# Low halves moved to GpSimd in three places, keys projected ahead of queries, and two heads alternating in an attention product, in a one-core float32 program of three transformer blocks

## The chip, the cores and the metric

The kernel runs on 1 core of one Trainium2 chip. The metric is device microseconds of one execution. Before the change three runs took 3091.12, 3094.21 and 3099.16 us, with a median of 3094.21.

## The reference

Everything is float32, with 256 tokens and a width of 1024. The first block is one layer with four branches, merged by gates, and a gated feed-forward network:

```
h = rms(x)
y_fox = softmax(q k / 8 + cum_f[q] - cum_f[k], causal) v    # 16 heads of 64, "forgetting" attention
y_lru = RG-LRU(h)                                           # a convolution and a linear recurrence
y_sb  = stick-breaking attention(h)                         # 16 heads of 64
y_mem = attention(h, 256 memory tokens)                     # 4 heads of 256
x += (sum_n sigmoid(h Wg_n) * (y_n Wb_n)) Wout
x += (silu(conv(h2 W1)) * (h2 W2)) Wdown
```

The second block has two layers over two streams, the 256 tokens and 256 context tokens, with shifts and scales from a modulation vector (ada):

```
h, hc = modulate(rms(x)), modulate(rms(ctx))
q, k, v, ... = split(h @ w_in), and the same of hc          # in the last layer hc gives only keys and values
ya = neighbourhood attention(q; keys of ctx and of x)       # 8 heads of 64, 512 keys
yb = differential attention(q; keys of ctx and of x)        # 4 heads of 2 x 64, 512 keys
yc = gMLP(u, v)
x += gate * merge(ya, yb, yc);   in layer 0 also ctx += ...
x += gate * mixture of 16 experts(x);  in layer 0 also for ctx
```

## The kernel before

One program of five instruction streams (TensorE `pe`, ScalarE `act`, VectorE `dve`, GpSimd `pool`, SyncE), written out by hand from line 2350 on. They meet at a barrier (`barrier`, L408) between stages: each stream drains, adds 1 to `stage_done`, and waits until all four have. The stages in their order: loads and norm; Q, K and V of the forgetting attention; its rounds; the recurrence; stick-breaking; memory; the first merge; the output projection; the feed-forward network; then for each layer the projection of K, Q and V (`proj2`), neighbourhood attention, in layer 0 context attention, differential attention (in layer 0 again for the context), gMLP, merge, output, router, experts.

**Weights.** They come as 621 slots of 1 MB through `ring`, four slots of two pieces (128 x 1024 words). SyncE issues a slot's load when both of its old pieces have been reported used. Most pieces are multiplied in three fp32r matmuls so that the result is as exact as float32 (`three`): high half times high half, high times low, low times high. So each such piece takes three steps: ScalarE rounds it to its high half (`split_hi`, L421, into one of four buffers `piece_hi`), VectorE subtracts to get the low half (`split_lo`, L428, into `ring_lo`), TensorE multiplies (L481 to L483; `piece_of` waits for the low half). 378 pieces are split so; the experts' pieces are not.

**Order.** Nothing is scheduled by a program: each stream's order is the order of the code. `split_ahead` is called on ScalarE and VectorE each time a piece is passed (`next_piece`), and puts the halves of the pieces up to `AHEAD = 3` further at that point of the stream. Both streams pass a piece at the read of its bank (`read_bank`), whichever of them reads it. So VectorE's low half stands between a bank's read and what comes next, and waits there for ScalarE's high half. GpSimd has little to do: it issues its own loads at some barriers, makes four products for the forgetting attention's mask and bias (L1133), adds squares in norms (L893) and low halves of the routed activations (L2094).

**Attention rounds.** A round is two heads (64 rows of the array each) and 256 queries in two tiles. `att_pe` runs on TensorE, per round: `scores` (L657), `turn` (transposes of the probabilities, L672), `product` with V (L682), and at two places a piece or two of other projections (`also`). On the others: ScalarE's exponentials (L726) and copies of the transposed (L741), VectorE's maxima (L787), reciprocals (L792) and probabilities (L796; in differential attention L799 subtracts the second map). The forgetting rounds are written apart (L1154 to L1234; L1173 is their product, L1234 their probabilities), 8 rounds of two heads. Differential attention has 4 rounds a layer and stream, neighbourhood attention 4.

**The layers' first stage, `proj2`.** `main_norm_dve` normalises the columns chunk by chunk (8 chunks of 128 rows): L938 scales, L944 gives the low half, of each of the two streams of 256 columns. `first_banks` takes three pieces at once, chunk by chunk of the norm (`ready`). Then one bank a piece (`fm_banks`), and last V (`tm_tile`). Queries came first: four banks of 512 columns in layer 0, of 256 in layer 1 (the context has no queries there), then four banks of keys of 512 columns. In layer 1 the norm of the context stream was made after the first chunks, between the banks of Q (`second_chunk_dve`, `norm_hi_act`), and TensorE waited for it ahead of K (`both`).

## Time and profile before

| | |
|---|---|
| three runs | 3091.12, 3094.21, 3099.16 us |
| profiled execution | 3091.37 us |
| its span | 3089.2 us |
| mean granted TensorE clock | 0.944 |
| TensorE busy | 2607.8 us, 84% of the span |
| VectorE busy | 1175.6 us, 38% |
| ScalarE busy | 877.1 us, 28% |
| GpSimd busy | 90.4 us, 3% |
| DMA | 669.40 MB, mean 217 GB/s |
| stages the change touches, us from the span's start | forgetting rounds 139.1 to 219.9; first merge 457.4 to 690.4; layer 0 proj2 931.4 to 1013.9, neighbourhood attention to 1097.4, context to 1140.1, differential to 1201.8, the same for the context to 1240.8; layer 1 proj2 2130.0 to 2215.4, neighbourhood attention to 2321.1, differential to 2380.5 |

How to read it: the span is the time from the first to the last instruction of the profiled execution, and its own time lies 2.2 us above it. Busy times are sums over an engine's instructions. A wait in the trace is idle time just before an instruction, put down to what came last before it; L numbers are lines of the kernel. A group of rows "x16" is as many instructions, and its time is from the first one's start to the last one's end. Matmuls are pipelined and overlap in the records. One float32 matmul of the attention rounds leaves two records.

### The profile page before, as it was taken

The numbers are of one execution on the slowest core, as the hardware profiler recorded it, in microseconds if no ns is written. First come the engines' busy times: TensorE is split into PE (matmuls) and PEld (weight loads), VectorE is DVE, ScalarE is ACT, GpSimd is POOL, SyncE is SP. The second block draws the span as 40 slices with busy tenths as digits, with TensorE's granted clock in tenths as the row PEclk, the third lists the DMA queues.
The fourth block names the chain that finished last, engine by engine and source line by source line (L and its number), as shares of the span: only waits on it lengthen the run. The fifth ranks groups of instructions, "written<-read, shape, count | busy, mean of one in ns | idle before, by whom it ended". The sixth has DMA issues, their size and how long they took to land.

```text
span 3089.2 us, 37382 instructions
## 1 busy us (share of the span) xinstructions
PE 2607.8 (84%) x14760; PEld 1784.8 (58%) x14760; DVE 1175.6 (38%) x1628; ACT 877.1 (28%) x1348; POOL 90.4 (3%) x78
## 2 busy tenths in 40 slices
PE   5889989999998988899787778886897987778786
PEld 5688868888996677588552222223676973222222
DVE  4557534456754645544430001014355651000001
ACT  4455533344443333322220000003234431000001
POOL 1100000000010000000110000001000001000000
PEclk8899989999999999899979999998898988999999
DMA  4434217764542111122469999995212435999996
GB/s 160 149 123 164 99 66 272 268 235 143 186 159 108 62 52 55 42 95 96 160 240 417 400 399 392 416 410 213 73 64 79 160 141 242 413 405 411 419 409 271
DMA packets 92949, 669.40 MB, mean 217 GB/s; under 512 B 10320, under 2 KB 10496, under 8 KB 12800
## 3 DMA queue, kind: packets, MB, share of 16 engines
q1 hardware_dynamic: 90256, 654.67, 54.1%
q0 software_dynamic: 2272, 11.52, 1.1%
q8 instruction: 115, 1.88, 0.2%
q10 hardware_dynamic: 272, 1.05, 0.1%
q14 instruction: 34, 0.28, 0.0%
HBM read 666.13 MB, written 1.06 MB: 216 GB/s over the span
## 4 chain that ended last, share of the span: by engine, by line
PE 44%; DMA 27%; DVE 7%; ACT 4%; issue 3%; DVEq 1%; SPq 0%; POOL 0%; ACTq 0%; POOLq 0%; PEldq 0%; PEld 0%
DMA ring<-in_stream 27%; PE ps L481 10%; PE ps L483 10%; PE ps L482 10%; PE ps L2186 7%; PE ps L496 2%; ACT piece_hi L421 1%; PE ps L682 1%; DVE WK L796 1%; DVE ring_lo L428 1%; ACT WK L726 1%; DVE small L787 1%; PE ps L672 1%; PE ps L657 1%; PE ps L494 1%
## 5 line engine op out<-in xcount | busy, mean ns | idle before, releaser
L2186 PE MATMUL ps<-ring,WK 128*64 128x512 f32 x3072 | 728.3, 603 | 167.0 <-DMA ring<-in_stream 143.2
L481 PE MATMUL ps<-A,piece_hi 128*128 128x256 f32 (+1 forms) x1952 | 624.3, 320 | 72.2 <-DVE A L944 26.4
L428 DVE TENSOR_TENSOR ring_lo<-ring,piece_hi 128x1024 fp32r<-128x1024 f32 x378 | 466.1, 1237 | 450.0 <-ACT piece_hi L421 449.1
L482 PE MATMUL ps<-A,piece_hi 128*128 128x256 f32 (+1 forms) x1952 | 610.8, 313 | 0.0
L483 PE MATMUL ps<-A,ring_lo 128*128 128x256 f32 (+1 forms) x1952 | 609.8, 312 | 0.0
L2186 PEld LDWEIGHTS ps<-ring,WK 128*64 128x64 f32 x3072 | 193.6, 136 | 667.7 <-DMA ring<-in_stream 370.5
L421 ACT ACTIVATE piece_hi<-ring 128x1024 fp32r<-128x1024 f32 x378 | 391.9, 1053 | 271.7 <-DMA ring<-in_stream 109.3
L481 PEld LDWEIGHTS ps<-A,piece_hi 128*128 128x128 f32 x1952 | 383.3, 196 | 116.2 <-issue 82.1
L482 PEld LDWEIGHTS ps<-A,piece_hi 128*128 128x128 f32 x1952 | 383.9, 197 | 18.3
L483 PEld LDWEIGHTS ps<-A,ring_lo 128*128 128x128 f32 x1952 | 382.6, 196 | 18.5
L2306 DVE TENSOR_TENSOR WK<-WK,ps 128x512 f32<-128x512 f32 x32 | 22.0, 687 | 630.1 <-PE ps L2186 630.1
L481 PE MATMUL ps<-WKR,piece_hi 128*128 128x256 f32 (+1 forms) x624 | 188.6, 302 | 4.7 <-DVE WKR L589 2.6
L482 PE MATMUL ps<-WKR,piece_hi 128*128 128x256 f32 (+1 forms) x624 | 187.5, 300 | 0.0
L483 PE MATMUL ps<-WKR,ring_lo 128*128 128x256 f32 (+1 forms) x624 | 187.4, 300 | 0.0
L2272 ACT ACTIVATE WK<-ps 128x512 f32<-128x512 f32 x32 | 19.1, 597 | 552.3 <-PE ps L2186 552.2
L481 PE MATMUL ps<-piece_hi,A 128*128 128x256 f32 (+1 forms) x480 | 158.7, 331 | 5.2 <-DVE WK L1851 5.2
L482 PE MATMUL ps<-ring_lo,A 128*128 128x256 f32 (+1 forms) x480 | 155.5, 324 | 0.0
L483 PE MATMUL ps<-piece_hi,A 128*128 128x256 f32 (+1 forms) x480 | 155.2, 323 | 0.0
L2254 DVE COPY WK<-ps 32x512 f32<-32x512 f32 x48 | 32.7, 682 | 272.1 <-PE ps L2186 271.9
L481 PEld LDWEIGHTS ps<-WKR,piece_hi 128*128 128x128 f32 x624 | 119.9, 192 | 18.7 <-issue 15.1
L483 PEld LDWEIGHTS ps<-WKR,ring_lo 128*128 128x128 f32 x624 | 120.1, 192 | 3.8
L482 PEld LDWEIGHTS ps<-WKR,piece_hi 128*128 128x128 f32 x624 | 120.0, 192 | 3.8
(266 smaller groups left out, 2433.1 us busy)
## 6 DMA issues: line engine op xcount, KB each, us to landing
ring<-in_stream SPq DMA_DIRECT2D x621, 1024.0 KB, 7.7
WK<-in_na_bias POOLq DMA_DIRECT2D x2, 2048.0 KB, 8.0
WK<-cum_scratch POOLq DMA_DIRECT2D x1, 2048.0 KB, 9.5
const<-in_const SPq DMA_DIRECT2D x1, 1267.0 KB, 12.0
WK<-in_x SPq DMA_DIRECT2D x1, 1024.0 KB, 5.5
WK<-in_mem SPq DMA_DIRECT2D x1, 1024.0 KB, 9.4
WK<-cum_scratch POOLq DMA_DIRECT2D x1, 1024.0 KB, 14.3
WK<-in_lru_w POOLq DMA_DIRECT2D x1, 1024.0 KB, 5.9
```

Of the source, the lines that this page charges most:

```text
L421: nc.scalar.activation(piece_hi[:, no % 4, :], ring[:, slot, at:at + PIECE], ACT.Copy).then_inc(hi_done[no % 4], 1)
L428: nc.vector.tensor_tensor(ring_lo[:, slot, at:at + PIECE], ring[:, slot, at:at + PIECE], f32(piece_hi[:, no % 4, :]), ALU.subtract).then_i ...
L481: nc.tensor.matmul(out_, l[0], r[0], start=first, stop=False)
L482: nc.tensor.matmul(out_, l[0], r[1], start=False, stop=False)
L483: return nc.tensor.matmul(out_, l[1], r[0], start=False, stop=last)
L494: last = nc.tensor.transpose(ps[0:rows, b, at:at + n], l, r)
L496: last = nc.tensor.matmul(ps[0:rows, b, at:at + n], l, r, start=(k == 0), stop=(k == len(pairs) - 1))
L657: last = nc.tensor.matmul(dst[:, a, qt, :], l, m, start=(j == 0), stop=(j == len(pairs) - 1))
L672: last = nc.tensor.transpose(ps[:, b, col % 512:col % 512 + P], t[:, a, qt, k * P:(k + 1) * P], ident)
L682: last = nc.tensor.matmul(ps[rows, at["y_bank"] + col // 512, col % 512:col % 512 + T], l, m, start=(j == 0), stop=(j == len(pairs) - 1))
L2186: last = nc.tensor.matmul(ps[64 * n:64 * n + 64, bank, :], lhs, piece[:, n * 512:n * 512 + 512], start=(k == 0), stop=(k == DC - 1))
L2254: return copy(YE[row:row + CAP, s, e // 4, half * 512:half * 512 + 512], ps[64 * half + CAP * s:64 * half + CAP * (s + 1), 6 + e % 2, :])
```

## The change

1. A table `GPS_LOW` marks 120 of the 378 split pieces, by their number among the split: 24 to 39 (the forgetting rounds), 88 to 151 (the first merge), and 20 in each layer, from the 13th split piece of the layer on (keys and queries of differential attention, 4 of its values, 8 of the gates). VectorE and ScalarE go past them as before, but GpSimd makes their low halves. `lows` does this in its stream: at each barrier it first makes those that ScalarE had made high halves of by that barrier (`ahead_of`), and at two places of each layer it is called ahead of a wait.
2. `att_pe`: in the score loop the query tile is the outer loop. In the product two heads take turns (`heads_beside=2`), matmul by matmul, for the attention of pairs; differential and memory attention keep one head after the other (`heads_beside=1`).
3. `proj2`: the norm always makes both streams, keys come first, then queries, then values; the stream of weights has the same order. `second_chunk_dve` and the norm between the banks of Q are gone.

```diff
+GPS_LOW = np.zeros(PIECES + 64, bool)
+def _mark_low():
+    split = np.array(SPLIT_AT)
+    block = 226
+    layer = MIX_PIECES
+    for lo, hi in ((24, 40), (88, 152), *((block + l * layer + 12, block + l * layer + 32) for l in range(LAYERS))):
+        GPS_LOW[split[lo:hi]] = True
...
         def barrier(eng, cur):
+            if cur.who == "act":
+                ahead_of.append(cur.s)
+            if cur.who == "pool":
+                lows(eng, cur)
             eng.drain().then_inc(stage_done, 1)
...
-        def split_lo(dve, cur):
+        def split_lo(eng, cur):
...
+            if cur.who == "dve":
+                nc.vector.tensor_tensor(to, of, hi, ALU.subtract).then_inc(lo_done[no % 4], 1)
+            else:
+                nc.gpsimd.tensor_tensor(to, of, hi, ALU.subtract).then_inc(lo_done[no % 4], 1)
             cur.s += 1
+        def lows(pool, cur):
+            while cur.s < ahead_of[cur.stage]:
+                if GPS_LOW[cur.s]:
+                    split_lo(pool, cur)
+                else:
+                    cur.s += 1
...
                 elif cur.who == "dve":
-                    split_lo(eng, cur)
+                    if GPS_LOW[cur.s]:
+                        cur.s += 1
+                    else:
+                        split_lo(eng, cur)
...
-                for a in range(2):
-                    for qt in range(2):
+                for qt in range(2):
+                    for a in range(2):
...
-                for a, rows, col, pairs in at["pv"](r):
-                    for j, (l, m) in enumerate(pairs):
-                        last = nc.tensor.matmul(ps[rows, at["y_bank"] + col // 512, col % 512:col % 512 + T], l, m,
-                                                start=(j == 0), stop=(j == len(pairs) - 1))
+                parts = at["pv"](r)
+                width = at["heads_beside"]
+                for at_ in range(0, len(parts), width):
+                    for j in range(kc):
+                        for rows, col, pairs in parts[at_:at_ + width]:
+                            last = nc.tensor.matmul(ps[rows, at["y_bank"] + col // 512, col % 512:col % 512 + T], *pairs[j],
+                                                    start=(j == 0), stop=(j == kc - 1))
...
-        def proj2_pe(pe, cur, nq, ready, both):
-            first_banks(pe, cur, in_a()(nq), nq, ready)
-            fm_banks(pe, cur, in_a()(nq), nq, BC - 3)
-            both()
-            fm_banks(pe, cur, in_a()(2 * T), 2 * T, BC)
+        def proj2_pe(pe, cur, nq, ready):
+            first_banks(pe, cur, in_a()(2 * T), 2 * T, ready)
+            fm_banks(pe, cur, in_a()(2 * T), 2 * T, BC - 3)
+            fm_banks(pe, cur, in_a()(nq), nq, BC)
             tm_tile(pe, cur, 0, 4)
-        def proj2_read(eng, who, cur, nq, beside):
-            for c in range(BC):
-                copies(eng, who, cur, lambda j: Q2[:, j, 0:nq], 1, nq, HD ** -0.5, first=c)
-                beside(c)
+        def proj2_read(eng, who, cur, nq):
             copies(eng, who, cur, lambda j: K2[:, j, :], 4, 2 * T)
+            copies(eng, who, cur, lambda j: Q2[:, j, 0:nq], 4, nq, HD ** -0.5)
             copies(eng, who, cur, lambda j: V2[:, j, :], 4, BW, tm=True)
...
                 barrier(pool, cur)
+                lows(pool, cur)
                 pool.wait_ge(loads, 16 * (n_loads + 1))
                 barrier(pool, cur)
...
+                lows(pool, cur)
                 pool.wait_ge(loads, 16 * (n_loads + 4))
```

VectorE in a forgetting round, where L1221 adds the bias to the scores, L1223 and L1224 take the maxima, L1231 and L1234 make the probabilities, L576 copies a bank of other projections. Before:

```order
L1221 TENSOR_TENSOR WK<-ps,WK 128x768
L1223 TENSOR_REDUCE small<-WK 128x2
L1224 TENSOR_REDUCE small<-WK 128x2
L428 TENSOR_TENSOR ring_lo<-ring,piece_hi 128x1024
L1231 RECIPROCAL small<-small 128x4
L1234 TENSOR_TENSOR WK<-WK,small 128x2x256
L1234 TENSOR_TENSOR WK<-WK,small 128x2x128
L576 TENSOR_SCALAR WK<-ps 128x256
L428 TENSOR_TENSOR ring_lo<-ring,piece_hi 128x1024
```

VectorE in the same round now (the code's lines have moved by 36 to 40):

```order
L1261 TENSOR_TENSOR WK<-ps,WK 128x768
L1263 TENSOR_REDUCE small<-WK 128x2
L1264 TENSOR_REDUCE small<-WK 128x2
L1271 RECIPROCAL small<-small 128x4
L1274 TENSOR_TENSOR WK<-WK,small 128x2x256
L1274 TENSOR_TENSOR WK<-WK,small 128x2x128
L612 TENSOR_SCALAR WK<-ps 128x256
```

Both low halves have left VectorE's round; nothing else of it moved.

GpSimd from the mask and bias of the forgetting attention to the load for the context (`L1127` to `L2688` before). Before:

```order
L1127 DMA WK<-cum_scratch 128x16x128
L1133 TENSOR_TENSOR WK<-WK,const 128x4x256 x4
L2681 DMA WK<-in_lru_w 128x2048
L2688 DMA WK<-in_ctx 128x2x1024
```

GpSimd there now:

```order
L1167 DMA WK<-cum_scratch 128x16x128
L1173 TENSOR_TENSOR WK<-WK,const 128x4x256 x4
L454 TENSOR_TENSOR ring_lo<-ring,piece_hi 128x1024 x16
L2709 DMA WK<-in_lru_w 128x2048
L454 TENSOR_TENSOR ring_lo<-ring,piece_hi 128x1024 x64
L2716 DMA WK<-in_ctx 128x2x1024
```

L454 is GpSimd's low half. Sixteen stand behind the four products, the first three of them ahead of the barrier before the forgetting rounds, and 64 ahead of the merge's end. In the layers 11 and 9 such rows stand in layer 0, and 15 and 5 in layer 1, on the two sides of the loads for the gMLP.

VectorE in layer 1's `proj2`, from the norm's reciprocal (L954 before) on. Before:

```order
L954 RECIPROCAL WK<-WK 128x512
L938 SCALAR_TENSOR_TENSOR WK<-XT,gmod,WK 128x256 x2
L944 SCALAR_TENSOR_TENSOR A<-WK,MOD,A 128x256
...
L944 SCALAR_TENSOR_TENSOR A<-WK,MOD,A 128x256 x2
L428 TENSOR_TENSOR ring_lo<-ring,piece_hi 128x1024
L938 SCALAR_TENSOR_TENSOR WK<-XT,gmod,WK 128x256 x2
L944 SCALAR_TENSOR_TENSOR A<-WK,MOD,A 128x256
L576 TENSOR_SCALAR WK<-ps 128x256
L428 TENSOR_TENSOR ring_lo<-ring,piece_hi 128x1024
L938 SCALAR_TENSOR_TENSOR WK<-XT,gmod,WK 128x256
L944 SCALAR_TENSOR_TENSOR A<-WK,MOD,A 128x256
```

VectorE there now:

```order
L994 RECIPROCAL WK<-WK 128x512
L978 SCALAR_TENSOR_TENSOR WK<-XT,gmod,WK 128x256 x4
L984 SCALAR_TENSOR_TENSOR A<-WK,MOD,A 128x256 x2
L978 SCALAR_TENSOR_TENSOR WK<-XT,gmod,WK 128x256 x2
...
L984 SCALAR_TENSOR_TENSOR A<-WK,MOD,A 128x256 x4
L452 TENSOR_TENSOR ring_lo<-ring,piece_hi 128x1024
L612 TENSOR_SCALAR WK<-ps 128x512
L452 TENSOR_TENSOR ring_lo<-ring,piece_hi 128x1024 x2
L612 TENSOR_SCALAR WK<-ps 128x512
```

The norm of the second stream (L938 and L944 of it) has moved from behind and between the first banks' reads to their front, two instructions of each kind for a chunk; the first read is now of a bank of 512 columns.

## Rows read from the trace of the kernel before

**Rows 1.** The page: busy time, share, instructions; and one costly group of instructions

```profile
PE 2607.8 (84%) x14760; PEld 1784.8 (58%) x14760; DVE 1175.6 (38%) x1628; ACT 877.1 (28%) x1348; POOL 90.4 (3%) x78
L428 DVE TENSOR_TENSOR ring_lo<-ring,piece_hi 128x1024 fp32r<-128x1024 f32 x378 | 466.1, 1237 | 450.0 <-ACT piece_hi L421 449.1
```

**Rows 2.** Stretches: us; PE, PEld, DVE, ACT, POOL busy; clock, DMA share, GB/s

```profile
139.10:219.90 80.80, 70.56 (x560) 63.84 (x560) 45.84 (x72) 42.27 (x105) 0.00 (x0) 0.92 0.26 93
457.40:690.40 233.00, 220.79 (x1752) 195.46 (x1752) 114.11 (x139) 85.98 (x102) 0.00 (x0) 0.98 0.67 250
931.40:1013.90 82.50, 69.93 (x292) 56.14 (x292) 34.91 (x52) 24.26 (x36) 0.56 (x1) 0.94 0.27 101
2130.00:2215.40 85.40, 63.68 (x292) 52.77 (x292) 34.92 (x52) 24.58 (x36) 0.55 (x1) 0.84 0.25 88
```

**Rows 3.** PE's waits (total, times, longest): forgetting, merge 1-2, context, differential 0, neighbourhood 1, differential 1

```profile
PE ps L1165 <- DVE WK L1234: 8.5, 6, 5.4
...
PE ps L481 <- DVE ring_lo L428: 5.3, 9, 0.8
PE ps L1733 <- DVE ROWS L1769: 4.4, 2, 2.3
...
PE ps L672 <- DVE WK L796: 3.6, 2, 2.4
...
PE ps L672 <- DVE WK L799: 8.4, 4, 4.2
...
PE ps L481 <- DVE WK L1851: 5.2, 1, 5.2
...
PE ps L672 <- DVE WK L799: 8.1, 4, 4.2
```

**Rows 4.** PE's timeline in layer 1's proj2: start, us, engine, instruction, [idle before]

```profile
2140.65 0.55 PE L481 MATMUL ps<-A,piece_hi 128*128 128x256 f32 x1 [7.92 <-DVE A L944]
...
2153.49 0.36 PE L481 MATMUL ps<-A,piece_hi 128*128 128x256 f32 x1 [2.15 <-DVE ring_lo L428]
...
2167.33 0.80 PE L481 MATMUL ps<-A,piece_hi 128*128 128x512 f32 x1 [9.60 <-DVE A L944]
...
2213.01 0.39 PE L483 MATMUL ps<-piece_hi,A 128*128 128x512 f32 x1
```

**Rows 5.** PE's timeline in layer 0's proj2, first and last matmuls

```profile
942.23 0.77 PE L481 MATMUL ps<-A,piece_hi 128*128 128x512 f32 x1 [8.84 <-DVE A L944]
...
962.65 0.47 PE L481 MATMUL ps<-A,piece_hi 128*128 128x512 f32 x1 [1.72 <-DVE ring_lo L428]
...
1011.28 0.39 PE L482 MATMUL ps<-ring_lo,A 128*128 128x512 f32 x1
1011.51 0.39 PE L483 MATMUL ps<-piece_hi,A 128*128 128x512 f32 x1
```

**Rows 6.** PE's timeline: product and scores of neighbourhood attention, product of a forgetting round

```profile
1044.21 2.86 PE L682 MATMUL ps<-WK 128*64 128x256 f32 x16
1047.01 1.99 PE L657 MATMUL ps<-WK 64*128 64x512 f32 x8
...
152.90 0.87 PE L1173 MATMUL ps<-WK 128*64 128x256 f32 x8
```

**Rows 7.** GpSimd (timeline; a group) and VectorE (timeline) with two operands of SBUF

```profile
121.42 12.32 POOL L1133 TENSOR_TENSOR WK<-WK,const 128x1024 f32<-128x1024 f32 x4 [13.17 <-DMA WK<-cum_scratch]
...
L2094 POOL TENSOR_TENSOR A<-WK,A 128x1024 fp32r<-128x1024 f32 x6 | 14.4, 2433 | 75.5 <-ACT A L2079 75.5
...
122.10 6.15 DVE L428 TENSOR_TENSOR ring_lo<-ring,piece_hi 128x1024 fp32r<-128x1024 f32 x2 [2.32 <-ACT piece_hi L421]
```

**Rows 8.** ACT's and VectorE's timeline in a differential round of layer 0

```profile
1149.13 1.07 ACT L421 ACTIVATE piece_hi<-ring 128x1024 fp32r<-128x1024 f32 x1
...
1149.75 2.29 DVE L796 TENSOR_TENSOR WK<-WK,small 128x2048 f32<-128x2048 f32 x1
```

**Rows 9.** VectorE's timeline in a forgetting round

```profile
172.49 1.22 DVE L428 TENSOR_TENSOR ring_lo<-ring,piece_hi 128x1024 fp32r<-128x1024 f32 x1 [3.15 <-ACT piece_hi L421]
```

More of the change, by code:

```diff
@@ L422, in split_hi @@
             cur.s += 1
[L424 removed]
+        def split_lo(eng, cur):
             no, slot, at = int(SPLIT_NO[cur.s]), cur.s // 2 % R, cur.s % 2 * PIECE
[L427 to L430 removed]
+            eng.wait_ge(hi_done[no % 4], cur.split_use(cur.s, 1))
+            to, of, hi = ring_lo[:, slot, at:at + PIECE], ring[:, slot, at:at + PIECE], f32(piece_hi[:, no % 4, :])
+            if cur.who == "dve":
+                nc.vector.tensor_tensor(to, of, hi, ALU.subtract).then_inc(lo_done[no % 4], 1)
+            else:
+                nc.gpsimd.tensor_tensor(to, of, hi, ALU.subtract).then_inc(lo_done[no % 4], 1)
+            cur.s += 1
+        def lows(pool, cur):
[4 more added lines that the diff above has]
+                    cur.s += 1
         def split_ahead(eng, cur):
@@ L838, in save @@
                 return y[:, r, y0:y0 + T], ps[:, 4, 0:T]
-            return dict(n=n, nk=nk, per=per, y_bank=4, diff=diff, bias=bias, qk=qk, pv=pv, save=save)
+            return dict(n=n, nk=nk, per=per, y_bank=4, heads_beside=1 if diff else 2, diff=diff, bias=bias, qk=qk, pv=pv, save=save)
         YT = wk(6400 + 6144, 4, DC, T)
@@ L1263, in mem_save @@
             return (YT[:, 3, 4 * r:4 * r + 4, :].rearrange("p (b c) t -> p b (c t)", b=2), ps[:, 6:8, :])
-        mem_att = dict(n=2, nk=T, per=0, y_bank=6, diff=False, bias=None, qk=mem_qk, pv=mem_pv, save=mem_save)
+        mem_att = dict(n=2, nk=T, per=0, y_bank=6, heads_beside=1, diff=False, bias=None, qk=mem_qk, pv=mem_pv, save=mem_save)
         SB_B = [wk(at, 2, SB) for at in (0, 2 * SB)]
@@ L2421, in _ @@
                 main_norm_pe(pe, cur, SQ_DOWN if layer == 0 else SQ_BACK, 2 * T)
-                x_all = cur.base("x") + 2 * DC
-                proj2_pe(pe, cur, n, ready=norm_ready(pe, cur, 2 * T, streams=n // T), both=lambda: pe.wait_ge(x_lo, x_all))
+                proj2_pe(pe, cur, n, ready=norm_ready(pe, cur, 2 * T))
                 barrier(pe, cur)
@@ L2512, in _ @@
                 shift = lambda c, s: MOD[:, layer * MODC + c, s:s + 1]
-                main_norm_act(act, cur, steps, 2 * T, shift=shift, streams=n // T)
-                proj2_read(act, "act", cur, n, beside=lambda c: [norm_hi_act(act, cur, 2 * c + j, 1, shift, True)
-                                                                 for j in range(2)] if n == T else None)
+                main_norm_act(act, cur, steps, 2 * T, shift=shift)
+                proj2_read(act, "act", cur, n)
                 barrier(act, cur)
@@ L2605, in _ @@
                 gain, shift = lambda c, s: gmod[:, c, s:s + 1], lambda c, s: MOD[:, layer * MODC + c, s:s + 1]
-                main_norm_dve(dve, cur, steps, 2 * T, gain, shift=shift, streams=n // T)
-                def beside(c):
-                    if n == T:
-                        for j in range(2):
-                            second_chunk_dve(dve, cur, 2 * c + j, gain, shift)
-                        if c == BC - 1:
-                            second_chunk_dve(dve, cur, DC, gain, shift)
-                proj2_read(dve, "dve", cur, n, beside)
+                main_norm_dve(dve, cur, steps, 2 * T, gain, shift=shift)
+                proj2_read(dve, "dve", cur, n)
                 barrier(dve, cur)
@@ L2798, in _stream @@
         w = x["w_in_2"][l]
-        for at, f in ((4, fm), (0, fm), (1, tm), (5, fm), (2, fm), (3, wide), (7, wide), (6, wide)):
+        for at, f in ((0, fm), (4, fm), (1, tm), (5, fm), (2, fm), (3, wide), (7, wide), (6, wide)):
             f(w, at * BW, (at + 1) * BW)
```

11 lines of the change are left out of this document (5 added, 6 removed).

## Prediction, made before the result was known

> **What bounds the kernel now.** I read the page's busy times first [rows 1]: TensorE is busy for 2607.8 of 3089.2 us, GpSimd for 90.4. GpSimd is all but idle, VectorE is busy for 38%, and of that 466 us are low halves at 1.24 us each. TensorE sets the time, so an edit is worth what it takes out of TensorE's own work or out of the waits between its instructions. Between its barriers the kernel is a row of stages, so next I read the stretches [rows 2]: in the first merge TensorE is busy for 220.8 of 233.0 us, in the first stage of layer 1 (the one that makes K, Q and V) for 63.7 of 85.4, where the granted clock is 0.84. Last, what TensorE waits for in the stages that the change touches [rows 3]. Those waits are short. What can be won is a few us in each place.
>
> The sum is made against the profiled execution's own 3091.37 us; the median of the three runs is 2.8 us above it, and I add these at the end. A measurement of this kernel tells a difference of about 0.3%, 9.3 us, from none.
>
> **Keys ahead of queries.** In layer 0 both have 512 columns and the norm already covers both streams: the order of two equal blocks of work changes, cost 0. In layer 1 K has 512 columns and Q 256. Before, TensorE starts on three Q banks at 2140.65, waits 2.15 us for a low half, and at 2167.33 has waited 9.60 us for the second stream's norm, which VectorE makes between other work [rows 4]. After, the norm makes both streams first, as in layer 0, and the first three banks are K banks. Layer 0 is therefore the pattern: first matmul 942.23, a wait of 1.72 for a low half, last matmul 1011.5 + 0.39, no second wait for the norm [rows 5]: 69.7 us for eight banks of 512 columns and V. In layer 1 four of the eight have 256 columns. A bank is 24 matmuls; those of 512 columns start 0.23 us apart (1011.28 and 1011.51, [rows 5]), those of 256 take 220.79 / 1752 = 0.126 in the merge [rows 2]: 24 × 0.104 = 2.5 us less each, 10.0 for four. The first matmul comes later by the second stream's share of the first chunk, two VectorE instructions of 0.48: 2141.6. So 2141.6 + 69.7 - 10.0 = 2201.3; I add 1.7 for the lower clock of this stage (0.84 against 0.94 in layer 0 [rows 2], a tenth of some 17 us of first banks), which gives 2203.0 against 2213.4 before: **-10.4**. Bounds: -13 if the clock rises as in layer 0 and more of the first banks' columns run at full rate; -7 if K's three wide banks are fed by the norm chunk by chunk (8 chunks of 4 × 0.48 = 15.4 us, against 16 to 18.7 us of matmuls) and so wait inside.
>
> **Heads taking turns in the product.** With 512 keys a product is 8 matmuls, 16 records of 256 columns, in 2.86 us [rows 6]. The 8 records of the forgetting rounds, where two heads' matmuls already alternate on the two column halves of the array, take 0.87. Sixteen at that pace would be 1.74; I take 1.95, since four more matmuls in a chain may not all pair up. Eight rounds have 512 keys (four in each layer): 8 × 0.9 = **-7.2**. Bounds: 0 if order has no part in it, -9.0 at 1.74. The product runs between work that waits for it, so what it sheds I count in full. Products with 256 keys, memory and differential attention: 0 (short already, or unchanged by `heads_beside=1`).
>
> **Score loop, query tile outside.** 8 records of 512 columns take 1.99 us in the old order [rows 6], as many columns as 16 of 256, for which 2.86 is the price without turns and 1.74 the one with full pairing. So the two heads, on separate halves of the rows, run beside each other already: 0, bounds 0 and -0.25 × 8 = -2.
>
>
> **120 low halves move to GpSimd.** Price: GpSimd's nearest instruction, two operands of 1024 words into fp32r, takes 2.43 us alone, VectorE 1.24 [rows 7, 1]. Where both engines run two-operand instructions from SBUF they slow each other: GpSimd's four at 121.42 took 12.32, 3.1 each, and two of VectorE's low halves beside them 6.15, 3.1 each instead of 1.24 [rows 7]. So a VectorE instruction with two SBUF operands that meets a GpSimd low waits up to about 2.1 us, and GpSimd's own low then takes 3.3.
> [...]
>
> - *Forgetting rounds, 16.* VectorE's order has a low half ahead of the probabilities, and it stood 3.15 us waiting for the high half while the exponentials were done [rows 9]. That goes. TensorE's waits on L1234 are 8.5 in all, but the first, before the loop is running, is 5.4 [rows 3] and stays. The other 3.1 I take as gone: **-3**. Bounds -3, +8 (eight rounds, each 1 us of L1234 meeting GpSimd).
> - *First merge, 64.* Waits on low halves 5.3 and on L1769 (VectorE, ROWS) 4.4 are 9.7 together [rows 3]. A low half comes 1.2 us later, but no longer stands before VectorE's reads of full banks, which free banks and ring slots. I take half: **-5**. Bounds -10; +10, if GpSimd at 3.3 a piece is later than the 2.9 us that TensorE takes for a piece of 256 columns (24 × 0.12), in one piece of three: 64 / 3 × 0.45.
> - *Layer 0: context attention, differential attention.* Context attention waits 3.6 for L796 [rows 3]: **-2**. In differential attention VectorE runs L796 (2.29 us, [rows 8]), then L799, then the lows, and TensorE waits 8.4 in four rounds for L799 [rows 3]. If GpSimd takes the port between L796 and L799, L799 is 2.1 late: first round 2.1, later rounds have VectorE's saved 1.22 per low half against it: **+2**. Bounds -4, +8.4.
> - *Layer 1.* Neighbourhood attention waits 5.2 for L1851, behind lows in VectorE's order: **-2**; differential attention 8.1 in four rounds [rows 3], here with five lows left to GpSimd only: **-2**. Bounds -8, +8.4.
> - *Stage ends.* GpSimd reaches each barrier behind the lows of the pieces ahead. At both layers' first stages the last high half releases 2.43 instead of 1.24: **+1.3** in layer 1, counting layer 0's as covered by half and layer 1's likewise. Before the forgetting rounds GpSimd has 4 × 3.1 from 121.42 [rows 7], then three lows, 133.7 + 3 × 2.43 = 141.0, or 138.4 if its four shrink to 2.4 without VectorE's lows beside them; the stage ends at 139.1 [rows 2]: 0, bounds 0, +2. GpSimd's weight loads behind its lows are wanted a stage later: 0.
>
> Sum: -10.4 - 7.2 - 3 - 5 - 2 + 2 - 2 - 2 + 1.3 = -28.3, so 3063.1, and with the 2.8 to the median **3066**.
>
> **Rivals.**
> 1. *Slower: the port.* GpSimd's lows start just before L796, L799 and L1234 in most rounds, because ACT makes the high half right after the exponentials [rows 8]. Eight differential rounds × 2.1 = 16.8, three exposed L796 waits × 2.1 = 6.3, eight forgetting rounds × 1 = 8, merge +10: +41; less 17.6 for the two TensorE edits, plus 1.3: +25, **3119**. For it: every meeting in rows 7 was paid in full. Against it: VectorE has long idle stretches, and most meetings will be with instructions that nobody waits for. It decides from about 13 paid meetings on (13 × 2.1 = 28). Chance 0.11.
> 2. *The low halves come out at nothing*, gains eaten by meetings: only 17.6 remain, less 1.3: **3078**. Chance 0.17.
> 3. *The waits go entirely*: 5 more in the merge and 8 in the attention rounds (what is left of 8.4, 8.1 and 5.2 in rows 3, half of it): **3053**. Chance 0.10.
> 4. *A TensorE edit doesn't do what it says*: K's wide banks wait for the norm inside, or 2.86 stays 2.86. 7 to 10 us less gained: **3075**; both, 3083. Chance 0.12.
> 5. The forecast, within 3057 to 3075: chance 0.50.
> 6. *Scores gain by turns what the products gain*, 0.9 in each of 24 rounds of pair and differential attention (two matmuls of one head in a row keep the other head's half of the array empty): 22 more, **3044**. Against it, the 1.99 in rows 6. Chance 0.03, out of case 3's 0.10.
> The Trainium skill, "TensorE: Matmul & The Clock Gate", section "The mechanism", has matmuls start and end strictly in program order, which is case 6; that the trace's pairs overlap in the old order speaks against taking it so far.
>
> **Numbers.** Cases 3 and 5 are faster by over 9.3 us (0.60 together with case 6), case 2 nearly always (0.15 of 0.17), case 4 mostly (0.09 of 0.12): 0.84, of which I move 0.04 to the other side for errors in the sum that the cases don't name. Same: 0.02 + 0.03 + the mild end of case 1, 0.03, + 0.02 = 0.10; slower 0.10. The range runs from 3048, between cases 3 and 6, to 3087, where both TensorE edits fail or half of case 1 happens.
>
> **What the profile after would show.** Right: in layer 1's first stage no wait on the norm after the first; that stage about 75 us long instead of 85.4; 16-record products at about 1.95; no row for TensorE waiting on L1769 in the merge, and the merge about 228 us; VectorE's lows at 258 and GpSimd's 120 at 2.4 to 3.3. Wrong: waits of TensorE on L796/L799 (now L836/L839) longer than before by 2 us a round; merge over 235 us with waits on GpSimd's ring_lo; products unchanged; the wait in layer 1 only moved into the first three banks.

## The result, and the profile after

The changed kernel took 3069.82 us (median of 5 runs, 3053.02 to 3078.14), against 3091.42 us before (5 runs, 3087.41 to 3099.16). The ratio is 0.9918, with a 95% interval of 0.9889 to 0.9947: 0.8% faster. The medians of the two lie 21.6 us apart, a ratio of 0.9930; the ratio with the interval is the one to go by. The forecast was 3066 in a range of 3048 to 3087, a ratio of 0.991 to the median then known. A second session with the changed kernel (`after_again`, below) gave 0.9883 (0.9860 to 0.9905), with medians 38.0 us apart. The two intervals overlap, and the forecast's ratio lies in the first and 0.0004 above the second.

The page of the changed kernel, the busy times (engine, us, share, instructions) and the two groups of low halves (busy us, mean ns, idle before):

```profile
PE 2606.0 (85%) x14760; PEld 1782.5 (58%) x14760; DVE 1082.0 (35%) x1508; ACT 877.0 (29%) x1348; POOL 397.9 (13%) x198
L452 DVE TENSOR_TENSOR ring_lo<-ring,piece_hi 128x1024 fp32r<-128x1024 f32 x258 | 314.5, 1224 | 247.2 <-ACT piece_hi L443 246.8
L454 POOL TENSOR_TENSOR ring_lo<-ring,piece_hi 128x1024 fp32r<-128x1024 f32 x120 | 310.2, 2601 | 689.2 <-ACT piece_hi L443 689.2
```

Against [rows 1] GpSimd has 307 us more to do, VectorE 94 less, although 120 low halves of 1.24 are 149: part of the rest is VectorE's own two-operand instructions getting longer beside GpSimd's (80 additions in the merges, L1580 before and L1620 now, from 40.4 to 56.1 us; L839, which was L799, from 12.6 to 22.7; 16 products in the neighbourhood stages, L1889, from 6.6 to 17.7). TensorE's busy time is the same within 2 us.

The stages of the changed kernel as stretches, in the order of forgetting rounds, merge, layer 0 proj2, layer 0 differential attention, layer 1 proj2 (columns as in [rows 2]):

```profile
138.60:216.10 77.50, 70.37 (x560) 64.15 (x560) 32.28 (x59) 42.37 (x105) 30.87 (x13) 0.92 0.28 97
454.30:683.30 229.00, 216.42 (x1752) 192.16 (x1752) 61.99 (x78) 85.82 (x101) 152.29 (x61) 1.00 0.67 254
927.30:1011.00 83.70, 70.33 (x292) 56.40 (x292) 31.35 (x49) 24.25 (x36) 7.70 (x4) 0.94 0.29 104
1130.50:1195.30 64.80, 55.16 (x336) 46.49 (x336) 30.66 (x22) 22.50 (x47) 14.99 (x5) 0.86 0.09 33
2126.60:2202.10 75.50, 62.09 (x292) 50.54 (x292) 30.80 (x49) 23.82 (x36) 7.68 (x4) 0.88 0.29 103
```

And TensorE's waits in the changed kernel (total, times, longest), the answers to [rows 3] in the same order: forgetting rounds, merge, context, layer 0 differential, layer 1 neighbourhood and differential attention:

```profile
PE ps L1205 <- DVE WK L1274: 5.4, 1, 5.4
...
PE ps L517 <- POOL ring_lo L454: 10.2, 16, 1.4
...
PE ps L708 <- DVE WK L836: 1.5, 2, 1.3
...
PE ps L708 <- DVE WK L839: 9.1, 4, 3.9
...
PE ps L517 <- DVE WK L1888: 2.3, 1, 2.3
...
PE ps L708 <- DVE WK L839: 6.5, 3, 3.1
```

The stages from barrier to barrier, in us, taken from the profiles:

| stage | forecast | before | after | keys only | turns only | lows only |
|---|---|---|---|---|---|---|
| forgetting rounds | -3 | 80.8 | 77.6 | 80.9 | 81.5 | 77.8 |
| first merge | -5 | 232.9 | 229.0 | 233.5 | 234.6 | 229.0 |
| layer 0 proj2 | +0 | 82.6 | 83.7 | 82.7 | 82.9 | 85.1 |
| neighbourhood | -3.6 | 83.4 | 79.9 | 83.5 | 79.4 | 83.4 |
| context | -2 | 42.8 | 39.6 | 42.8 | 41.8 | 39.7 |
| differential | +2 | 61.6 | 64.8 | 61.5 | 61.0 | 64.8 |
| layer 1 proj2 | -9.1 | 85.4 | 75.5 | 72.4 | 87.3 | 88.1 |
| neighbourhood | -5.6 | 105.7 | 99.6 | 107.3 | 103.3 | 101.1 |
| differential | -2 | 59.4 | 56.8 | 58.3 | 59.2 | 57.9 |
| these nine | -28.3 | 734.6 | 706.5 | 722.9 | 731.0 | 726.9 |

The nine stages lost 28.1 us, and 29.9 in the second profile of the changed kernel. The profiled execution as a whole (3073.91 us) is only 17.5 us below the one before, because stages that the change does not touch came out longer in it: the experts of layer 0 504.1 against 499.5, of layer 1 489.6 against 487.4, the feed-forward network's second half 74.4 against 71.7. In the second profile of the changed kernel the first of these is 498.6. Layer 1's experts took 487.4 and 491.7 us in two profiles of the kernel before.

One end of a stage is not in this table. Ahead of the forgetting rounds the barrier waits for GpSimd's first three low halves too. In the profile above they are done before VectorE is, and cost nothing. In three of the nine profiles with these marks (`lows_only`, `merge_on_vector`, `best`) the rest of that stage was done some 3 us earlier, as it also was in the second profile of the kernel before, and GpSimd reached the barrier 4 to 5 us behind VectorE. In `best` VectorE was there at 135.3, and GpSimd's three low halves ran until 139.9:

```profile
132.94 6.93 POOL L454 TENSOR_TENSOR ring_lo<-ring,piece_hi 128x1024 fp32r<-128x1024 f32 x3
```

### The profile page after: what moved, and what is told of

It is laid out like the page before. It is cut to its first block, busy times and chain, and to the rows that moved or that the text cites. A ratio compares the mean times of both kernels' runs of the same rounds, so it can differ in the third digit from the quotient of the medians.

```text
span 3072.1 us, 37385 instructions
## 1 busy us (share of the span) xinstructions
PE 2606.0 (85%) x14760; PEld 1782.5 (58%) x14760; DVE 1082.0 (35%) x1508; ACT 877.0 (29%) x1348; POOL 397.9 (13%) x198
## 3 DMA queue, kind: packets, MB, share of 16 engines
q10 hardware_dynamic: 272, 1.05, 0.1%
## 4 chain that ended last, share of the span: by engine, by line
PE 48%; DMA 26%; DVE 6%; ACT 4%; issue 3%; POOL 1%; DVEq 1%; SPq 0%; POOLq 0%; ACTq 0%; PEldq 0%; PEld 0%
DMA ring<-in_stream 26%; PE ps L517 11%; PE ps L518 11%; PE ps L519 11%; PE ps L2223 7%; PE ps L532 2%; PE ps L722 1%; POOL ring_lo L454 1%; PE ps L693 1%; DVE WK L836 1%; ACT WK L766 1%; PE ps L708 1%; DVE small L827 1%; PE ps L530 1%; ACT piece_hi L443 1%
## 5 line engine op out<-in xcount | busy, mean ns | idle before, releaser
L517 PE MATMUL ps<-A,piece_hi 128*128 128x256 f32 (+1 forms) x1952 | 622.4, 319 | 64.8 <-DVE A L984 17.7
L517 PEld LDWEIGHTS ps<-A,piece_hi 128*128 128x128 f32 x1952 | 381.8, 196 | 108.3 <-issue 83.7
L452 DVE TENSOR_TENSOR ring_lo<-ring,piece_hi 128x1024 fp32r<-128x1024 f32 x258 | 314.5, 1224 | 247.2 <-ACT piece_hi L443 246.8
L454 POOL TENSOR_TENSOR ring_lo<-ring,piece_hi 128x1024 fp32r<-128x1024 f32 x120 | 310.2, 2601 | 689.2 <-ACT piece_hi L443 689.2
L933 POOL TENSOR_TENSOR WK<-WK 128x512 f32<-128x512 f32 (+1 forms) x42 | 47.7, 1136 | 1577.7 <-ACT WK L928 1576.6
L517 PEld LDWEIGHTS ps<-WKR,piece_hi 128*128 128x128 f32 x624 | 120.6, 193 | 22.1 <-issue 18.4
```

Of the source, the lines that this page charges most:

```text
L452: nc.vector.tensor_tensor(to, of, hi, ALU.subtract).then_inc(lo_done[no % 4], 1)
L454: nc.gpsimd.tensor_tensor(to, of, hi, ALU.subtract).then_inc(lo_done[no % 4], 1)
L517: nc.tensor.matmul(out_, l[0], r[0], start=first, stop=False)
L933: ins = nc.gpsimd.tensor_tensor(sq[:, 0, 0:n], sq[:, 0, 0:n], sq[:, c, 0:n], ALU.add)
```

## The experiments

### The three parts apart

`keys_only` is the changed kernel without marks, without turns and with the old score loop; `turns_only` and `lows_only` likewise leave one part each.

```diff
-    for lo, hi in ((24, 40), (88, 152), *((block + l * layer + 12, block + l * layer + 32) for l in range(LAYERS))):
+    for lo, hi in ((0, 0),):
```

> Only the third part of the change: keys ahead of queries, all low halves on VectorE, heads one after the other. If the parts are worth what the stages of the changed kernel show, layer 1's first stage goes from 85.4 to about 73.6 us (75.5 as in the changed kernel, less the 1.9 us that GpSimd's low half ended later than VectorE), no wait for the norm after the first, and every other stage stays within 0.5 us, the experts' apart: total 11 to 12 us less than before, ratio about 0.996. Rival (the gain of that stage was made by the other two parts): the stage stays near 85.

Measured: ratio 0.9963 (0.9946 to 0.9980), 3084.89 us against 3095.53. Layer 1's first stage is 72.4 us long, 1.2 less than expected (why is said further down), layer 1's neighbourhood stage 107.3, 1.6 more than before, and its differential attention 58.3, 1.1 less, which I had not expected; the other attention stages are as before. Outside the nine stages layer 1's experts took 500.1 us in this profile, 12.7 more than before, which is why the profiled run alone, 3094.30 us, shows no gain.

> Only the second part: query tile outside in the scores, heads taking turns in the product. Theory: products with 512 keys 1.95 instead of 2.86 us, scores unchanged at 1.99; both neighbourhood stages 3.6 us shorter (83.4 to 79.8, 105.7 to 102.1), nothing elsewhere: total 7.2 less, ratio about 0.9977. Rival (scores gain by turns as well): also the context and differential stages shorter, by 3 us or more each, and total 20 or more less.

Measured: ratio 0.9975 (0.9961 to 0.9990), 3087.70 us. TensorE's timeline in a neighbourhood round (start, us, instruction):

```profile
1047.93 1.95 PE L722 MATMUL ps<-WK 128*64 128x256 f32 x16
1049.81 1.99 PE L693 MATMUL ps<-WK 64*128 64x512 f32 x8
```

Product 1.95, as expected to the last digit, and scores 1.99 as before. The two neighbourhood stages are 4.0 and 2.4 shorter, where 3.6 each was expected. The other stages were not all still: context attention is 1.0 shorter, the merge 1.7 and layer 1's first stage 1.9 longer. Why was not tested.

The products with 256 keys show what a shorter run of matmuls on one half of the columns costs. In context attention two matmuls (four records) of one head stand in a row before the change and take turns after it. First the kernel before, then `turns_only`:

```profile
1112.01 1.09 PE L682 MATMUL ps<-WK 128*64 128x256 f32 x8
...
1112.01 1.08 PE L722 MATMUL ps<-WK 128*64 128x256 f32 x8
```

> Only the first part: 120 low halves on GpSimd. Theory from the stages of the changed kernel: forgetting rounds 3.2 less, merge 3.9 less, layer 0 first stage 1.1 to 1.9 more, context attention 3.2 less, differential attention of layer 0 3.2 more, layer 1 first stage 1.9 more, neighbourhood 2.5 less, differential 2.6 less: about 8 to 9 less in all, ratio about 0.997. Rival (low halves worth nothing in sum): 0.999 to 1.001.

Measured: ratio 0.9971 (0.9952 to 0.9989), 3083.98 us. The three ratios multiply to 0.9909, inside the change's own interval: the parts add up as far as the noise lets one see, and by the medians each is worth 8 to 12 us (10.6, 7.8 and 11.6). By the nine stages of one profile each they are worth 11.7, 3.6 and 7.7, 23.0 in all against 28.1 for the three together.

### A second profile of the kernel before

> The kernel before, unchanged, for a second profile. Theory (the merge's gain is the clock, which fell after the two waits of 2.1 and 2.3 us on ROWS): the same two waits and the same two dips of the clock, TensorE busy about 220.8 of 233 us in the merge. Rival (the dips are chance): the merge of this profile is shorter by up to 4 us at a clock of 1.00 with the same waits. The stages that the change does not touch (experts, feed-forward) show how far a profile is from the next: I expect up to 5 us in the experts and under 0.5 us in the attention stages.

Measured: one run of 3091.79 us, and the merge 233.8 us long, with both waits on ROWS (4.4 us, as before). ROWS is the buffer to which VectorE copies a finished bank of the modulation vector (L1769) and which TensorE then turns (L1733). Layer 1's first stage is 86.5, 1.1 more than in the first profile, and its experts 4.3 more. The merge's stretches of 20 us around the two waits, and the one after:

```profile
515.00:535.00 20.00, 17.76 (x120) 14.90 (x120) 7.91 (x8) 8.65 (x11) 0.00 (x0) 0.83 0.64 249
575.00:595.00 20.00, 17.82 (x134) 15.00 (x133) 9.39 (x10) 7.49 (x9) 0.00 (x0) 0.91 0.66 238
595.00:615.00 20.00, 18.83 (x154) 15.84 (x153) 8.97 (x13) 5.23 (x6) 0.00 (x0) 1.00 0.73 287
```

In the changed kernel the same parts of the stage:

```profile
513.00:533.00 20.00, 19.31 (x157) 17.34 (x158) 4.80 (x6) 7.79 (x10) 13.57 (x6) 1.00 0.73 282
573.00:593.00 20.00, 19.03 (x154) 17.06 (x155) 4.62 (x6) 7.38 (x9) 13.35 (x6) 1.00 0.73 274
```

The reader is to compare the matmuls in 20 us, 120 and 134 against 157 and 154, and the clock, 0.83 and 0.91 against 1.00. A stretch's mean below 1.00 means that for a part of it the clock was at its lower level, 1.2 GHz instead of 2.4. At half the clock, 0.83 and 0.91 are about 6.8 and 3.6 us of 20 at the lower level. The dips are no chance: both come, with these two means, in all five merges with the low halves on VectorE (both profiles of the kernel before, `keys_only`, `turns_only` and `merge_on_vector`).

### Where the merge's gain is

> The changed kernel with the 64 low halves of the first merge back on VectorE. Theory (the merge's 3.9 us are the clock, not the waits: VectorE's low halves held back the two reads of ROWS, and the clock fell after those waits): the merge back at 233 to 234.5 us, two waits on ROWS of 2.2 each, about 5.5 us of waits on VectorE's low halves, and in 20 us slices the clock at 0.83 and 0.91 after the two waits on ROWS. Rival (the merge's gain came from elsewhere): the merge stays at 229 to 231.

```diff
-    for lo, hi in ((24, 40), (88, 152), *(...)):
+    for lo, hi in ((24, 40), *(...)):
```

Measured: merge 234.7 us in one run of 3072.10, and from the table of waits and the stretches:

```profile
PE ps L517 <- DVE ring_lo L452: 6.8, 11, 0.8
...
PE ps L1773 <- DVE ROWS L1809: 4.4, 2, 2.2
...
515.00:535.00 20.00, 17.80 (x120) 14.94 (x120) 7.81 (x7) 8.19 (x10) 0.00 (x0) 0.83 0.64 238
...
575.00:595.00 20.00, 17.78 (x133) 15.16 (x132) 9.19 (x10) 7.49 (x9) 0.00 (x0) 0.91 0.67 242
```

The waits and both dips are back: the 64 low halves are the cause of the merge's gain. VectorE's timeline before the change shows why it reads ROWS late: its low half stands ahead of that read and waits 3.73 us for the high half.

```profile
521.04 1.23 DVE L428 TENSOR_TENSOR ring_lo<-ring,piece_hi 128x1024 fp32r<-128x1024 f32 x1 [3.73 <-ACT piece_hi L421]
522.18 0.68 DVE L1769 COPY ROWS<-ps 128x512 f32<-128x512 f32 x1
```

> The changed kernel with only three of the merge's 64 low halves on GpSimd, those that stand just ahead of the three reads of ROWS in VectorE's order. Theory: no wait on ROWS, hence no dip of the clock, and the low halves at VectorE's 1.24 us instead of 2.6, so waits of about 5.5 instead of 10.2 us: merge about 224 to 225 us instead of 229.0. Rival 1 (it takes most of the 64 to free VectorE): merge 228 to 234 with waits on ROWS. Rival 2 (the period of a step is set by the loads, so that what one wait loses the next gains): merge 229.

```diff
-    for lo, hi in ((24, 40), (88, 152), *(...)):
+    for lo, hi in ((24, 40), (106, 107), (122, 123), (138, 139), *(...)):
```

Measured: merge 229.3 us in one run of 3080.07, not the 224 to 225 of the theory. Within a profile's scatter three low halves do what 64 do, and no more. The waits in it:

```profile
PE ps L517 <- DVE ring_lo L452: 6.7, 13, 0.8
...
PE ps L517 <- POOL ring_lo L454: 2.5, 2, 1.3
```

The waits on ROWS are gone, but the others grew to 9.2 us, as much in all as the 9.7 before and the 10.2 of the changed kernel. So rival 2 of this expectation holds for the waits: what one loses the next ones take up, however fast the low half is. What differs is the clock. One dip of 0.91 was left here, in the stretch with a 1.3 us wait on GpSimd's low half; a wait of 1.2 us, in the place of the first wait on ROWS, brought none.

All 64 on GpSimd are no sure way to a merge without a dip either. Of the seven profiles that have them, five took 228.3 to 229.0 us. The two others are `best` (231.4, below) and `diff_on_vector`, whose merge is that of the changed kernel and took 231.0. There TensorE waited 2.0 us for one low half:

```profile
593.00:613.00 20.00, 17.35 (x129) 14.35 (x128) 5.17 (x6) 6.49 (x8) 12.88 (x6) 0.91 0.62 227
```

### The port in the differential attention

"The port" stands for the way to SBUF that GpSimd and VectorE have in common. In layer 0's differential attention of the changed kernel, GpSimd's and VectorE's timelines in two rounds:

```profile
1140.71 3.91 POOL L454 TENSOR_TENSOR ring_lo<-ring,piece_hi 128x1024 fp32r<-128x1024 f32 x1 [16.06 <-ACT piece_hi L443]
1154.08 2.37 POOL L454 TENSOR_TENSOR ring_lo<-ring,piece_hi 128x1024 fp32r<-128x1024 f32 x1 [9.46 <-ACT piece_hi L443]
...
1140.13 2.29 DVE L836 TENSOR_TENSOR WK<-WK,small 128x2048 f32<-128x2048 f32 x1
1142.46 3.24 DVE L839 TENSOR_TENSOR WK<-WK 128x1024 f32<-128x1024 f32 x1
1145.63 2.28 DVE L827 TENSOR_REDUCE small<-ps 128x4 f32<-128x2048 f32 x1
...
1158.85 1.22 DVE L839 TENSOR_TENSOR WK<-WK 128x1024 f32<-128x1024 f32 x1
```

The low half is called at 1140.71 while L836 runs, and takes 3.91 instead of 2.37, as if it got through when L836 ends at 1142.42. L839 is called at 1142.46 and takes 3.24 instead of 1.22, as if it got through when the low half ends at 1144.62. In the next round the low half ran before L836, and both have their own price. This is what the Trainium skill, "SBUF — State Buffer", section "Who interferes with whom", calls an exclusive lock in order of issue, and here the trace agrees.

A VectorE instruction with a single operand in SBUF was held as well. L834, two words in each partition, takes 0.23 us elsewhere, and 1.05 here, until the low half of 1177.73 ends at 1180.08:

```profile
1177.73 2.35 POOL L454 TENSOR_TENSOR ring_lo<-ring,piece_hi 128x1024 fp32r<-128x1024 f32 x1 [7.61 <-ACT piece_hi L443]
...
1179.05 1.05 DVE L834 TENSOR_SCALAR small<-small 128x2 f32<-128x2 f32 x1
```

> The changed kernel with the low halves of the last 8 marked pieces of each layer (the gates', made in the differential attention) back on VectorE. Theory (in layer 0 GpSimd's low half takes the port between L836 and L839, and L839 is 2 us late in three or four rounds): L839 back from a mean of 2.5 to 1.22 us, layer 0's differential stage from 64.8 to 61.5 us, and layer 1's from 56.8 back to 58 to 59 us. Rival (the 3.2 us are the lower clock of that stage and not L839): 64 us or more with L839 at 1.22.

```diff
-    ... *((block + l * layer + 12, block + l * layer + 32) for l in range(LAYERS))
+    ... *((block + l * layer + 12, block + l * layer + 24) for l in range(LAYERS))
```

Measured: L839 (the group's count, busy us, mean ns), and in the changed kernel:

```profile
L839 DVE TENSOR_TENSOR WK<-WK 128x1024 f32<-128x1024 f32 x8 | 9.8, 1224 | 0.3
```

```profile
L839 DVE TENSOR_TENSOR WK<-WK 128x1024 f32<-128x1024 f32 x8 | 20.0, 2498 | 0.3
```

Layer 0's stage is 61.2, layer 1's 59.1, as the theory had it. But it also cost where I had expected nothing. Of the eight low halves only five are made in the differential attention; in layer 0 the other three are made in context attention, which went from 39.6 to 41.8 and waits 3.7 us for L836 again: this is where most of that stage's gain came from. Layer 0's neighbourhood stage went from 79.9 to 81.5 with the same eight low halves on GpSimd, at a mean clock of 0.94 against 0.96; why was not found. The single run took 3062.33 us.

TensorE's waits on L839 are 9.1 us in the changed kernel and 8.7 here, so the waits alone don't make the 3.6 us between the two. The rest is TensorE's own work at a lower clock. Stretches of 15 us, from 10 us into layer 0's stage, of the kernel before, `diff_on_vector`, the changed kernel and `ends_on_vector` (below):

```profile
1150.10:1165.10 15.00, 12.58 (x82) 9.43 (x80) 11.15 (x10) 5.72 (x13) 0.00 (x0) 1.00 0.19 70
...
1143.30:1158.30 15.00, 12.15 (x80) 9.09 (x76) 11.15 (x10) 5.65 (x13) 0.00 (x0) 1.00 0.20 70
...
1140.50:1155.50 15.00, 11.64 (x66) 10.31 (x67) 7.42 (x4) 5.32 (x12) 5.33 (x2) 0.77 0.00 0
...
1135.90:1150.90 15.00, 11.58 (x72) 10.03 (x72) 8.71 (x7) 5.51 (x12) 4.66 (x2) 0.89 0.13 44
```

Behind the late L839 of the first round the clock falls. That dip is in all seven profiles in which this L839 is late, and in none of the other six.

### The score loop

> The changed kernel with the old order in the score loop (head outside, query tile inside), turns in the product kept. Theory: the score records stay at 1.99 us for 8 of 512 columns and all stages within 0.5 us of the changed kernel. Rival (turns in the scores are worth something): context attention longer by 1 us, and the rounds with 512 keys by 0.2 us each or more.

Measured: 3070.81 us in one run; 8 records of 512 columns in 1.99, and the layers' attention stages within 0.1 us of the changed kernel. Memory attention, which uses the same loop, took 28.2 us against 27.5, inside the 26.5 to 28.2 of the thirteen profiles. The new order in the score loop does nothing that a profile shows.

```profile
1041.73 1.95 PE L722 MATMUL ps<-WK 128*64 128x256 f32 x16
1043.61 1.99 PE L693 MATMUL ps<-WK 64*128 64x512 f32 x8
```

### A version that puts twelve low halves back

> The changed kernel with only the first three of each layer's twenty low halves back on VectorE. Theory: layer 0's first stage 83.7 to 82.6 and layer 1's 75.5 to 73.6, its differential attention still 64.8. Rival: the neighbourhood stages behind them, which start with these low halves done, get longer by as much.

```diff
-    ... *((block + l * layer + 12, block + l * layer + 32) for l in range(LAYERS))
+    ... *((block + l * layer + 15, block + l * layer + 32) for l in range(LAYERS))
```

Measured, one run of 3057.61 us: the first stages are 83.0 and 74.9, the neighbourhood stages behind them 79.6 and 97.3 (99.6 before this edit). The rival is wrong: nothing was given back, layer 1's neighbourhood stage even gained 2.3. I had also expected layer 0's differential attention to stay at 64.8, and that was wrong: it took 60.9, though L839 is late there as before (3.25 us in two rounds) and TensorE waits 9.5 us for it. What differs is the clock, a mean of 0.94 over the stage against 0.86. Context attention ahead of it took 38.7 against 39.6, at a clock of 1.00 against 0.97. How long the clock stays down behind the same wait thus differs from one profile to another.

> The changed kernel with 12 low halves back on VectorE: the first three of each layer's twenty, which GpSimd makes late at the end of the layer's first stage, and in layer 0 the last five, which meet L839 in the differential attention. Theory: layer 0's first stage 83.7 to 82.6, its differential attention 64.8 to 61.5, layer 1's first stage 75.5 to 73 or 74, all else unchanged: 5.5 to 7 us less than the changed kernel, median some 3064, ratio to before about 0.990. Rival (what the stages lose is given back in the next stage, since pieces and buffers are as far ahead as they can be): within 2 us of the changed kernel.

```diff
-    ... *((block + l * layer + 12, block + l * layer + 32) for l in range(LAYERS))
+    ... *((block + l * layer + 15, block + l * layer + (27, 32)[l]) for l in range(LAYERS))
```

> The changed kernel unchanged, on the same chip as the version above and for a second profile: ratio to before 0.992 as measured, merge 229 us at a clock of 1.00 and with waits of 10 us on GpSimd's low halves, layer 0's differential attention 64.8.

Measured in the same session: `best` 3061.01 us, ratio 0.9894 (0.9871 to 0.9918); `after_again` 3058.48 us, ratio 0.9883 (0.9860 to 0.9905). In `after_again` the merge is 228.3 us with 9.2 us of waits on GpSimd's low halves, as expected, and layer 0's differential attention 62.7 instead of 64.8. The seven layer stages in question did what was expected, or better (layer 0's differential attention was to be 61.5, and layer 1's neighbourhood stage unchanged): 82.8, 79.5, 38.7 and 59.7 in layer 0, where `after_again` has 85.1, 79.8, 39.6 and 62.7, and 74.1, 97.3 and 56.7 in layer 1, against 75.6, 99.6 and 56.8. That is 10.4 us less in all. Yet the whole is not faster. In the profiles it was lost in stages that the edit leaves alone: the merge 231.4 against 228.3, layer 0's routing 67.2 against 63.0, its experts 504.9 against 498.6. The merge's part can be read. TensorE's waits in `best`'s merge and the stretches behind the longest of them:

```profile
PE ps L517 <- POOL ring_lo L454: 11.0, 15, 1.9
...
593.00:613.00 20.00, 16.92 (x130) 14.06 (x130) 5.86 (x6) 5.33 (x7) 13.82 (x6) 0.95 0.71 275
613.00:633.00 20.00, 19.14 (x152) 17.16 (x151) 3.50 (x6) 6.97 (x8) 11.18 (x6) 0.96 0.65 251
```

One low half came 1.9 us late, and the clock fell behind it. In `after_again` the same stretch has 149 matmuls at 1.00. I do not claim that `best` is better: by the timed runs it is the same as the changed kernel, and whether what the other stages lost in this profile is chance was not settled.

## Why the prediction was right, point by point

**The total: luck to some part.** The nine stages came out at -28.1 for -28.3, but single stages miss by up to 1.2 us either way and cancel, and the medians of the two sessions lie on both sides of the 3066 that was forecast (3069.82 and 3058.48).

**Keys ahead of queries: right, size and way.** The forecast had the first matmul 0.9 later than before, no second wait, and the last one ending 10.4 us earlier. TensorE's timeline in the changed kernel:

```profile
2139.24 0.77 PE L517 MATMUL ps<-A,piece_hi 128*128 128x512 f32 x1 [8.84 <-DVE A L984]
2160.28 0.47 PE L517 MATMUL ps<-A,piece_hi 128*128 128x512 f32 x1 [1.72 <-DVE ring_lo L452]
...
2198.89 0.39 PE L519 MATMUL ps<-piece_hi,A 128*128 128x512 f32 x1
```

From 2139.24 to 2199.28 are 60.0 us, against the 61.4 that the pattern of layer 0 [rows 5] and my surcharge for the clock gave. The waits of 8.84 and 1.72 are those of layer 0 to the last digit. Counted from the start of the stage the first matmul comes 2.0 us later than before, not 0.9, and the last one ends 10.7 earlier. Left alone (`keys_only`) the stage won 13.0 us; the changed kernel gives 3.1 of it back. 2.3 of that is TensorE's last matmul ending later into the stage, at a mean clock of 0.88 against 0.91. Only 0.8 is the end of the stage: it comes 2.8 us behind that matmul with the last low half on GpSimd, and 2.0 behind it with that low half on VectorE. The expectation of `keys_only` took 1.9 for this price, from a VectorE that no longer had a low half to make, and nothing for the 2.3 of the clock: 1.1 too much and 2.3 too little make the 1.2 by which it was off. Whether GpSimd's low halves bring the lower clock was not tested.

**Heads taking turns: right.** 2.86 to 1.95, eight times, 7.3 us; the sum had 7.2, and `turns_only` measured 7.8.

**Score loop: right at 0**, and case 6 is out. The Trainium skill, "TensorE: Matmul & The Clock Gate", section "The mechanism", has matmuls start and end in program order. No run here tests that. What the runs show is that two matmuls in a row on one half of the array cost nothing against turns, on row halves (1.99 both ways) as on column halves (1.09 and 1.08), and that four in a row on a column half cost 0.91 in 2.86. Four in a row on a row half were not run.

**Forgetting rounds: right.** -3 forecast, -3.2 measured, and of the waits on L1234 the first of 5.4 is what is left. The meetings that the bound of +8 feared did not come: L1274 takes a mean of 0.69 us for 512 words, as L1234 did. GpSimd's low halves begin when the probabilities (L1274, 170.10 to 171.13 in this round) are done:

```profile
170.10 1.03 DVE L1274 TENSOR_TENSOR WK<-WK,small 128x512 f32<-128x512 f32 x2
...
171.15 4.74 POOL L454 TENSOR_TENSOR ring_lo<-ring,piece_hi 128x1024 fp32r<-128x1024 f32 x2 [3.64 <-ACT piece_hi L443]
```

**First merge: right sum, wrong step.** The forecast was -5, half of the waits on low halves, 5.3, and on ROWS, 4.4. The profile shows -3.9, but the waits did not shrink: 9.7 before, 10.2 after, 9.2 with three low halves. What shrank is TensorE's busy time, 220.79 to 216.42 us, because the clock no longer fell. The step that failed is the one that took waits for the price of the edit ("no longer stands before VectorE's reads ... I take half"); their effect on the clock was the price. `merge_on_vector` and `merge_three` show that the waits on ROWS bring the dips, as far as removing them removes the dips (one smaller dip stayed in `merge_three`). Why the waits sum to the same in all versions was not tried; that the loads of the ring set the period is only argued.

**Layer 0: right in sign, the sizes in part by luck.** Context -3.2 for -2, of which 2.1 are waits. Differential +3.2 for +2 by the mechanism named, L839 late by 2.0; but TensorE's waits on it grew by 0.7 only, and the sum had no term for the clock. In the second profile of the changed kernel the stage is at +1.1 (62.7), with the same 9.2 us of waits on L839 and a clock of 0.91 instead of 0.86, and in `ends_on_vector` at -0.7. So of the 3.2 the port is under 1 us in waits, and the rest is the clock, which fell behind them.

**Layer 1: right.** Neighbourhood attention, the turns taken off, -2.5 for -2: the wait on L1851 (L1888 now) went from 5.2 to 2.3. Differential attention -2.6 for -2, with 1.6 less to wait on L839, though it is late in three of four rounds.

**Stage ends: right in the layers, not always before the forgetting rounds.** The end of the first stage comes 2.8 us behind TensorE's last matmul in both layers. In `ends_on_vector`, where that matmul ends within 0.1 us of the same time in the stage, it comes 2.0 behind. That is 0.8 a layer, 1.5 for both (unrounded), and the sum had 1.3. Layer 0's first stage as a whole came out 1.1 to 2.5 longer; what is more than 0.8 lies ahead of the last matmul. Before the forgetting rounds GpSimd's four took 9.40, then three in 6.96, until 137.6, ahead of 138.6: 0, as forecast; but in three other profiles, as said above, this end was paid with 4 to 5 us, beyond the bound of +2.

**Rival 1, slower by the port**, would have needed 13 paid meetings. L839 paid in five of eight rounds, L836 once (3.81 us in layer 0's neighbourhood stage; a mean of 2.39 for 2.29), L1274 not at all. The longer additions in the merges and L1889 met GpSimd too, but none of TensorE's waits in the table of waits is on them. In the rounds shown ScalarE's high half comes after the exponentials, so GpSimd is called when L836 already holds the port. It is L839 behind it that pays.

## What to carry to other kernels

Moving work from a waited-for engine to an idle one pays where it stood in the order ahead of something urgent and was itself waiting, not where it was merely busy: three of 64 low halves bought what the merge gained. Look at what stands next behind the moved instruction's new neighbour: here the second of two two-operand VectorE instructions in a row was the one that paid. Look also at the barrier behind it, which the slower engine may now reach last. And make the consumer with full-width work first when its input comes late in two parts: preparing both parts in one go cost 0.9 us of wait at the start and saved one of 9.6 in the middle.

## What the runs showed that I had not expected

A single wait in a stretch that is otherwise full can be dearer than its length. In the merge TensorE's clock fell after waits of 2.1 to 2.3 us on ROWS (to means of 0.83 and 0.91 over 20 us, 120 and 134 matmuls instead of 155), in `best` and `diff_on_vector` after one of 1.9 and 2.0 us, and in `merge_three` after one of 1.3. Sixteen waits of 0.2 to 1.4 us in the changed kernel, together longer than the ones before, left it at 1.00. The length of a wait therefore doesn't settle alone whether the clock falls: 1.3 us did it once, and 1.4 another time did not. In the merge the waits on ROWS, 4.4 us, came with 4.4 us more of busy time.

The other surprise is how far stages that share nothing with an edit move between profiles, 496.9 to 504.9 us in layer 0's experts, 486.5 to 500.1 in layer 1's and 62.9 to 69.1 in layer 0's routing. With single runs between 3053 and 3078 us for one kernel, a gain of 10 us shows in the stages' table long before it shows in the median.
